# Longer runs in DRAM for the expert weights of a two-block model, with their rows renumbered on chip, and another order at the end of the up product

## What is computed

```python
def expert_choice_ffn(x, router_w, wg, wu, wd):
    aff = jax.nn.softmax(jnp.einsum('bnd,de->bne', x, router_w).astype(jnp.float32), axis=-1)
    gate, idx = lax.top_k(aff.transpose(0, 2, 1), cap)        # 16 experts, 32 tokens each
    xg = x[bidx, idx]
    hid = jax.nn.silu(jnp.einsum('becd,edf->becf', xg, wg)) * jnp.einsum('becd,edf->becf', xg, wu)
    o = jnp.einsum('becf,efd->becd', hid, wd) * gate[..., None].astype(x.dtype)
    return jnp.zeros_like(x).at[bidx, idx].add(o)

# first part, layer l of 2 (the context stream xc only in layer 0)
x = x + g2 * expert_choice_ffn(rms_norm(x, norm2_g[l]) * (1.0 + sc2) + sh2, router_w[l],
                               exp_w_gate[l], exp_w_up[l], exp_w_down[l])
# second part, layer l of 2: D_FF = 2816
gt, up = jnp.split(jnp.einsum('bsd,df->bsf', x, w_ffn_up), [D_FF], axis=-1)
ffn = jnp.einsum('bsf,fd->bsd', jax.nn.silu(gt) * up, w_ffn_down)
x = _layernorm(DEEPNORM_ALPHA * x + ffn, ln2_g, ln2_b)
```

## Time and profile before

| | us |
|---|---|
| median of 3 runs | 3023.22 (3022.17 to 3023.78) |
| profiled execution | 3017.21 |
| its span | 3015.0 |
| PE busy | 2769.8 (92%) |
| DVE / ACT busy | 1188.0 (39%) / 590.4 (20%) |
| moved by DMA | 670.21 MB, mean 222 GB/s |

### The profile page before, as it was taken

One profiled execution on the slowest core, in us unless ns is written; L12 is line 12 of the kernel. 1 busy time (PEld: TensorE's weight loads), 2 busy tenths in 40 slices (PEclk: granted clock), 3 DMA queues, 4 the chain that ended last, 5 costly groups with the idle time before them and its releaser, 6 DMA issues.

```text
span 3015.0 us, 31181 instructions
## 1 busy us (share of the span) xinstructions
PE 2769.8 (92%) x12416; PEld 1542.1 (51%) x12416; DVE 1188.0 (39%) x2158; ACT 590.4 (20%) x1159; POOL 74.6 (2%) x125
## 2 busy tenths in 40 slices
PE   6998789999989998987777999999999999999998
PEld 3455554434334555433322586664454686664453
DVE  2545532222325453111111343343665444344674
ACT  1143211111101242101010114240110213330110
POOL 2100000000001000000000000001000000000000
PEclk9999889999999997988898999999999999999999
DMA  9414249999998346999999543224434432314341
GB/s 281 126 57 156 84 177 390 409 409 409 409 409 273 126 147 251 391 409 409 409 409 409 202 140 112 84 84 142 166 140 154 167 140 84 112 61 163 140 181 70
DMA packets 231807, 670.21 MB, mean 222 GB/s; under 512 B 8112, under 2 KB 18664, under 8 KB 231664
## 3 DMA queue, kind: packets, MB, share of 16 engines
q1 hardware_dynamic: 224848, 653.28, 57.4%
q0 software_dynamic: 6816, 14.94, 2.0%
HBM read 667.09 MB, written 2.90 MB: 222 GB/s over the span
## 4 chain that ended last, share of the span: by engine, by line
PE 67%; DMA 20%; DVE 6%; SPq 3%; ACT 2%; issue 2%; POOL 0%; DVEq 0%; ACTq 0%; POOLq 0%
DMA ring<-in_exp_w_up_dram 19%; PE bank L900 18%; PE bank L1585 8%; PE bank L1481 8%; PE bank L912 8%; PE bank L1645 4%; PE bank L1499 4%; PE bank L314 3%; PE bank L1121 3%; SPq L586 2%; PE bank L1173 1%; PE bank L1060 1%; PE bank L1321 1%; PE bank L1082 1%; PE bank L942 1%
## 5 line engine op out<-in xcount | busy, mean ns | idle before, releaser
L912 PE MATMUL bank<-ring,arena 128*64 128x512 f32 (+1 forms) x2992 | 598.1, 639 | 125.1 <-DMA ring<-in_exp_w_up_dram 100.9
L912 PEld LDWEIGHTS bank<-ring,arena 128*64 128x64 f32 (+1 forms) x2992 | 174.2, 129 | 528.9 <-issue 423.7
L900 PE MATMUL bank<-ring,arena 128*128 128x512 f32 (+1 forms) x764 | 318.1, 576 | 1.2 <-ACT arena L442 1.2
L1481 PE MATMUL bank<-ring,arena 128*128 128x512 f32 x640 | 296.0, 593 | 0.0
L1585 PE MATMUL bank<-ring,arena 128*128 128x512 f32 (+1 forms) x672 | 267.1, 557 | 3.8 <-issue 3.3
L900 PEld LDWEIGHTS bank<-ring,arena 128*128 128x128 f32 x764 | 144.5, 191 | 165.3 <-issue 163.2
L900 PE MATMUL bank<-arena,ring 128*128 128x256 f32 x1024 | 222.7, 379 | 0.0
L900 PEld LDWEIGHTS bank<-arena,ring 128*128 128x128 f32 x1024 | 193.5, 189 | 29.0 <-issue 0.9
L2658 DVE COPY arena<-bank 128x512 f32<-128x512 f32 x64 | 44.3, 692 | 404.1 <-PE bank L912 403.1
L1585 PEld LDWEIGHTS bank<-ring,arena 128*128 128x128 f32 x672 | 126.6, 190 | 137.6 <-issue 134.9
L1481 PEld LDWEIGHTS bank<-ring,arena 128*128 128x128 f32 x640 | 111.7, 191 | 91.8 <-issue 91.8
(11 more groups left out here) (341 smaller groups left out, 2807.0 us busy)
## 6 DMA issues: line engine op xcount, KB each, us to landing
ring<-in_exp_w_down_dram SPq DMA_DIRECT2D x64, 2048.0 KB, 20.7
ring<-in_exp_w_up_dram SPq DMA_DIRECT2D x63, 2048.0 KB, 23.8
ring<-in_exp_w_gate_dram SPq DMA_DIRECT2D x60, 2048.0 KB, 23.6
ring<-in_w_in_dram SPq DMA_DIRECT2D x42, 2048.0 KB, 7.7
ring<-in_ada_w_dram SPq DMA_DIRECT2D x24, 2048.0 KB, 11.4
ring<-in_w_ffn_up_dram SPq DMA_DIRECT2D x20, 2048.0 KB, 8.0
ring<-in_w_ffn_down_dram SPq DMA_DIRECT2D x10, 2048.0 KB, 8.1
ring<-in_w_out_dram SPq DMA_DIRECT2D x8, 2048.0 KB, 10.1
```

What stands on the lines that cost most here:

```text
L900: last = mm(o, lhs(k), rhs(k), start=start and k == 0, stop=stop and k == kt - 1)
L912: last = mm(U(us[c])[g * rows:(g + 1) * rows, :], lhs(k), rhs(i, c), start=(k < parts), stop=(k >= KT - parts))
L1481: last = mm(U(u)[:, :], T[:, k, t * P:(t + 1) * P], w[:, k, :], start=(k == 0), stop=(k == KT - 1))
```

## The change

1. Gate and up chunks: partition p now gets rows 2p and 2p + 1 of each half of the chunk, so that a run in DRAM is two rows. Down chunks: rows 4p to 4p + 3, a run of four rows. Number and size of the DMAs stay.
2. So that the products agree, the gather reads XN with a step of two elements, the fold reads the partial rows with a step of four elements, and gain and shift are brought into the new order once per layer: eight small products (16 instructions) in `last_ada`, one copy by DVE into `PAIRED`, and a wait on ACT for that copy.
3. Second part: the turn of tile 5 stands in place 1 instead of place 0, and DVE's order changes: `down_sums(0)` before the adds of the last tile, `down_sums(1)` behind them, `down_sums(2)` ahead of `hidden_sums(5)`.

```diff
+        PAIRED = SMALL[:, 58:90].rearrange("p (j g a s) -> p j g a s", j=2, g=2, s=2)
+        def paired(row, k):
+            return row.rearrange("p (a n j) -> p a j n", n=P, j=2)[:, k // 2, k % 2, :]
...
-                return w[l, q // 6, (q % 2) * CN:(q % 2 + 1) * CN, :].rearrange("(k p) n -> p k n", p=P)
+                return w[l, q // 6, (q % 2) * CN:(q % 2 + 1) * CN, :]
+            def load_rows(to, rows, what):
+                eng.dma_start(to.rearrange("p (a j) n -> p a j n", j=2),
+                              rows.rearrange("(a p j) n -> p a j n", p=P, j=2)).then_inc(sem[what], 16)
...
-                eng.dma_start(wide[s], expert_rows_of(l, q)).then_inc(sem[f"chunk{s}"], 16)
+                if q // 2 % 3 == 2:
+                    eng.dma_start(wide[s], expert_rows_of(l, q).rearrange("(p j) n -> p j n", p=P)).then_inc(sem[f"chunk{s}"], 16)
+                else:
+                    load_rows(wide[s], expert_rows_of(l, q), f"chunk{s}")
... (last_ada, PE)
                     gate_rows(1)
+                    u = bank_for(DENSE)
+                    for j in range(2):
+                        for half in range(2):
+                            for g, cols in enumerate((GAIN[1], SHIFT[1])):
+                                last = mm(U(u)[64 * half:64 * half + 64, 16 * j + 8 * g:16 * j + 8 * g + 8],
+                                          ident.rearrange("p (n j) -> p j n", j=2)[:, j, :],
+                                          cols.rearrange("p (a h) s -> p h a s", h=2)[:, half], start=True, stop=True)
+                    last.then_inc(full[u % BANKS], 1)
... (gather and gather_next)
-                                last = mm(U(u)[:, j * P:(j + 1) * P], XN[:, 2 * s + t, k * P:(k + 1) * P],
+                                last = mm(U(u)[:, j * P:(j + 1) * P], paired(XN[:, 2 * s + t, :], k),
... (fold)
-                                              parts[:, c, i * P:(i + 1) * P], FOLD[M], start=True, stop=True)
+                                              parts[:, c, :].rearrange("p (n j) -> p j n", j=4)[:, i, :], FOLD[M], start=True, stop=True)
... (down product, PE)
-                    if places[0] == 0:
+                    if places[0] == 1:
                         turn_hidden(5, [0, 1])
... (last_ada, ACT and DVE)
+                    u = ac.unit(lane=DENSE)
+                    nc.scalar.wait_ge(free[u % BANKS], ac.uses(u))
...
+                    u = landed(dv.unit(lane=DENSE))
+                    frees(v.tensor_copy(SMALL[:, 58:90], U(u)[:, 0:32]), u)
... (DVE, second part)
+                    if i == len(FF_WIDTHS) - 1:
+                        down_sums(0)
                     u_p7, u_p5, u_p6, u_p3, u_p4 = [dv.unit() for _ in range(5)]
...
-                        down_sums(0)
...
-                        down_sums(1)
...
+                down_sums(1)
                 nc.vector.wait_ge(sem["gate_silu"], dv.due("gate_silu"))
                 step(tt(part[1], part[1], part[3], ALU.mult), "hid_ready")
+                down_sums(2)
                 hidden_sums(5, [turned])
-                for place in range(2, 6):
+                for place in range(3, 6):
```

More of the change, by code:

```diff
@@ L603, in first_expert_loads @@
                         n = part.shape[1]
-                        eng.dma_start(part, expert_rows_of(l, RING + x)[:, k:k + n, :]).then_inc(sem[f"extra{x}"], 16)
+                        load_rows(part, expert_rows_of(l, RING + x)[k * P:(k + n) * P, :], f"extra{x}")
                         k += n
@@ L1708, in gathered @@
                 o, i = into[:, k, :, 32 * s:32 * s + 32], U(u)[:, j * P:(j + 1) * P].rearrange("p (e c) -> p e c", e=4)
-                g, b = GAIN[1][:, k, s:s + 1], SHIFT[1][:, k, s:s + 1]
+                g, b = (PAIRED[:, k % 2, i_row, k // 2, s:s + 1] for i_row in range(2))
                 if e is ac:
@@ L2223, in _ @@
                 u_first = ac.unit()
-                ac.unit()
+                ac.unit(6)
                 turned_hidden(5, [0, 1])
-                ac.unit(5)
                 row(SS2[:, 62:63], ones[:, 0:1], ACT.Sqrt, "scalar_step")
@@ L3051, in _ @@
                         up_sums(i + 1, 0)
-                    else:
-                        down_sums(0)
                     landed(u_p6)
@@ L3071, in _ @@
                     frees(tt(part[1], part[1], U(u_p4)[:, 0:n], ALU.add), u_p4)
-                u_p1, u_p2, turned, u_p7, u_p5, u_p6, u_p4, u_p3 = [dv.unit() for _ in range(8)]
+                u_p1, u_p2, u_p7, u_p5, u_p6, u_p4, u_p3, turned = [dv.unit() for _ in range(8)]
+                down_sums(1)
                 nc.vector.wait_ge(sem["gate_silu"], dv.due("gate_silu"))
                 step(tt(part[1], part[1], part[3], ALU.mult), "hid_ready")
+                down_sums(2)
                 hidden_sums(5, [turned])
-                for place in range(2, 6):
+                for place in range(3, 6):
                     down_sums(place)
```

## The result

The changed kernel takes 3056.1 us (median of 4 runs, 3053.2 to 3061.1), the kernel before on the same chip 3023.4 us: a ratio of 1.011 (95% interval 1.009 to 1.013), so **33 us slower**. The forecast was 2983, the range ended at 3032. The two differences are not the same, because the profiled execution of the kernel before lies 6 us under its median and that of the kernel after (3056.2) does not.

A forecast was written before the change was run, and what follows sets the result against it. The prediction took DMA to bound the expert stages and PE mostly the rest. Its terms, -27.3 + 2.8 - 15.6 = -40.1 us, took 3023.2 to 2983; the range of 8 in 10 was 2965 to 3032.

The forecast's parts named there:

- part 2: Expert stages and `last_ada`: stepped loads of fold and gather cost nothing, new products add 2.8 us in all.
- Rival (b): Expert fold: a 16-byte step halves the load rate, making the kernel slower; chance 0.19 with the doubled gather.
- plain form: Fold loads alone double, 3.65 us more per expert; layer 0 loses DMA's gain; +8.4 us, 3032.
- the 16 folds: Layer 0's expert stage: folds at half rate add 58.4 us on PE.
- the waits that PE gives up: Layer 0's expert stage: 26.6 us of PE waiting for DMA, set against the slower folds.
- with doubled gather, 3053: Layer 0: the loads of six gathers double too, 22 us, for a time of 3053.
- layer 1: priced at -14.2: Layer 1's expert stage: longer packets save 3.3% of 434 us, with slow folds hidden but for the last expert.
- Part 1: Expert stages of both layers: longer DMA runs cut the cost per packet, saving 27.3 us.
- the wait of PE that would be left in layer 0: Layer 0's expert stage: of 26.6 us of PE idle for DMA, 13.5 remain after the longer runs.
- Part 3: Second part's up product: new order removes two 5.8 us PE waits and the slow clock behind them, saving 15.6 us.
- The small terms: `last_ada`'s new products at 1.4 us per layer, 2.8 in all; the gather's step taken as free.
- the room, 26 ns per load: Layer 0: the fold may grow 13.5 us in 16 experts before it costs anything.

The follow-up runs named there:

- experiments 2: The kernel before with only the fold's loads at a step of four elements: 3089.4 us, ratio 1.022 (1.020 to 1.024).
- experiment 7: The kernel before with only the gather's loads at a step of two elements: 3018.1 us beside 3018.1, ratio 1.000 (0.999 to 1.001).
- experiment 1: The changed kernel with the fold reading contiguous pieces again (output not the reference's): 2974.7 us, ratio 0.984 (0.982 to 0.987) to the kernel before.
- experiment 3: The kernel before with only the longer DMA runs: 2993.5 us beside 3018.5, ratio 0.990 (0.988 to 0.992).
- experiment 4: The kernel before with only the new order at the end of the up product: 3004.3 us beside 3018.5, ratio 0.995 (0.993 to 0.997).
- the kernel with step 2: The changed kernel with down chunks in 8 KB runs and the fold at a step of two elements: 2982.5 us, ratio 0.987 (0.984 to 0.989).

## Why the prediction was wrong

**The step that failed** is one sentence of part 2: "I take 0" for the fold's stepped loads. Measured were 239 ns per load, 123 more than the 116 of the contiguous fold: a little above the upper end of the range beside it, "0 to 114 ns per load". The term was in the text, with its range, and the value chosen from it was the wrong end. The value was taken from loads of 8 columns, 96 against 89 ns, and from a read at a step of 8 bytes on one for 16. Neither was a guide to 16 bytes: at 8 bytes a full load of 128 columns pays no more than 7 ns either, and 8 and 16 bytes lie on different sides of the bend. The reason given beside it, that PE reads one float32 per column at a little over 1 element per ns in either case, was the thing in question; at a step of 16 bytes it reads 128 in 239 ns. (Whether the 7 ns of the small loads are a step's price stays open, as they differ in kind.) The prediction had in front of it a rule that says where the bend is, the Trainium skill (SBUF — State Buffer, "Door 1: The DMA port swizzle"): lines of 16 bytes, and full bandwidth only from two hits in a line on. The runs agree with it: 123 ns at two hits, 187 at 12 bytes, 239 at one hit. The same passage goes on to name 4 fp32 as how far one can stride for free, which by its own rule is one hit per line; the prediction doesn't mention it, and the measurement decides against it (239 ns). The two halves of the passage disagree on just this edit, and the two small rows spoke for it only by being small: that was reason for more than a chance of 0.19.

**Rival (b)** was the right mechanism and named the right sign. Its plain form gave +8.4 us and 3032. That is 31 us short of the 39.0 between the traces and 24 short of the measured median (the 6 us between the two were added to the forecast, and the kernel after doesn't have them). The terms are these:

- the 16 folds: priced at 58.4, measured 63.1;
- the waits that PE gives up: priced at 26.6, measured 26.5;
- the clock: not priced at all. Gather, scatter and turn behind slow folds cost 26.1 us (12.3 + 12.1 + 1.7). The form "with doubled gather, 3053" came near the measured 3056 by luck: the gather wasn't slow by its own step (experiments 2 and 7), and the scatter, which no step touches, was as slow;
- the products of `halved`: not priced, 4.7 us less. 1.4 of these are one chunk of the kernel before that ran at a low clock behind a wait for DMA (16 products in 5.07 us at 650.47, 3.65 for the others, the clock at 0.50 and 0.66 in the windows there); the rest is not traced;
- layer 1: priced at -14.2, measured -8.4. With the fold contiguous the same stretch is 1188.00 to 1620.61, 432.6 us, so -14.7: the price was right. The 6.3 us went to the slow folds of the first experts: from the first product to the first wait for a DMA the chain takes 57.7 us in the kernel after and 49.3 with the fold contiguous. The last fold's 3.6 came as priced.

**Part 1** was right, but for 0.3 us of rounding (3.3% of 401.5 and of 434 are 27.6 us, not 27.3). The line through 2 and 4 KB gave 421 and 427 GB/s and 29.75 us per expert; experiment 1 shows 29.7 and 422 to 424 GB/s, and experiment 3 is 25 us faster than before by the medians, 29 by the ratio, where 27.3 were forecast. The estimate from the Trainium skill (DMA: Bandwidth & Descriptors, "Why small descriptors are slow (HBM only)"), 3 cycles per packet and some 12 us, is too small here: the rate rose by 3.4% (409 to 423), not by 1.2 to 1.7. Also right was the wait of PE that would be left in layer 0, 13.5 us; experiment 1 has 12.2. In the kernel after this gain shows in layer 1 alone, since in layer 0 DMA is no longer late.

**Part 3** was right: 15.6 forecast, 15.1 in the traces, 15 (11 to 20, by the interval) in experiment 4, and the clock stays at 1.00 where it stood at 0.50.

**The small terms**: the new products take 1.05 us in layer 0 and 0.68 in layer 1 (1.4 each taken), the gather's step nothing that reaches the end (experiment 7). The forecast's sum was -40.1 with a fold that costs nothing. Experiment 1 is just that case, and gave -47 us by its ratio (-40 to -54) and -43.5 between the traces (2971.5 against 3015.0). The forecast's own range, 2963 to 3007, holds its 2974.7.

**The size of the mistake.** The prediction did name the room, 26 ns per load, up to which PE's waits in layer 0 would cover the fold. Step 2 (7 ns) is under it, step 3 (some 70 ns) is over it and step 4 far over. That the cover was thin is what made one line weigh more than the other two parts: in the kernel after it costs some 81 us (1.011 less 0.984), and in the kernel before, where the cover is 26.6 us of waits and not 12.2, it costs 67.

## What to carry to other kernels

When data is laid out anew for longer DMA runs, look for who reads it with a step afterwards, and put the step where it is free: here in the copy out of PSUM, not in the load of a stationary operand. Measure the step of such a load at its own size before it goes onto the path, or keep it to two float32, which cost 7 ns of 116 here; the rate at 8 bytes said nothing of the rate at 16. And look at rows that the change doesn't touch: here the slow fold had a second price, 26 us in the clock of what stands behind it.

## What the runs showed of the hardware

- Loads of a 128 x 128 float32 stationary operand, by step: 116 ns at 4 bytes, 123 at 8, 187 at 12, 239 at 16, 246 at 32, by the fold's length over its 32 loads.
- From 540 to 901 us PE is busy without a pause in two runs: with the doubled contiguous fold the granted clock is 1.00, with the stepped fold of the kernel after it is 0.90, and 0.50 in the second half of a fold and behind it.
- In the expert stages packets of 8 and 16 KB give 422 to 424 GB/s where 4 KB give 409; 8 KB throughout, in the kernel with step 2, gives 421:

```profile
GB/s 289 114 67 158 85 144 382 421 421 422 421 421 288 127 149 254 361 421 421 421 421 421 204 141 113 85 85 143 143 140 183 169 138 89 101 69 169 141 157 97
```

- ACT and DVE read a PSUM bank at a step of 4 float32 at no cost (585 and 692 ns for 128 x 512); with DVE's write to SBUF at a step of 128 float32 the copy takes 1050 ns.
